# Attention steps of the second layer two slots earlier, and the join of near and far keys begun from the maxima

## The chip, the cores and the metric

The kernel is one program on one core of a Trainium2 chip. The metric is device time in microseconds (us) of one execution; the kernel before takes 2042.96 us, the median of three runs (2039.75 to 2043.41). A core has five engines with a queue each, working side by side and ordered by semaphores: TensorE (PE in the profile; its weight loads are PEld) for matrix products and transposes, VectorE (DVE), ScalarE (ACT), GpSimd (POOL) and SyncE (SP), which issues most DMA transfers. Matrix products end in PSUM, which the kernel uses as eight banks; the rest lies in SBUF.

## The reference, cut to what matters

A two-layer transformer over 512 tokens of width 1024 in float32. Each layer is attention and then a mixture of 32 experts, two per token. The change lies in the attention of the second layer: eight heads of width 64, each over three groups of keys with stride 1, 4 and 16, joined by the groups' log-sum-exp:

```python
def dilated_attention(h, w_q, q_gain, w_o, kv_blocks, rel_bias):
    q = rmsnorm((h @ w_q).reshape(b, s, B_NUM_GROUPS, N_HEADS, B_HEAD_DIM), q_gain[:, None, :])
    for g, (window, dil) in enumerate(B_GROUPS):
        kb, vb = kv_blocks[g]
        logits = jnp.einsum('bnqhd,bnkhd->bnhqk', qb, kb) * scale
        logits = jnp.where(mask[None, :, None], logits + bias[None, None], -jnp.inf)
        lse = jax.nn.logsumexp(logits, axis=-1)
        p = jnp.exp(logits - lse[..., None])
        o = jnp.einsum('bnhqk,bnkhd->bnqhd', p.astype(vb.dtype), vb)
        ...
    w = jax.nn.softmax(jnp.stack(lses, axis=2), axis=2)
    o = jnp.einsum('bsgh,bsghd->bshd', w.astype(outs[0].dtype), jnp.stack(outs, axis=2))
    return o.reshape(b, s, B_OUT_WIDTH) @ w_o

def hier_moe(h, w_group, b_group, w_expert, b_expert, w_gate, w_up, w_down):
    ...   # which experts a token goes to depends on h, so on the attention before it
```

## The kernel before

The second layer's attention has a loop of slots, n = 0, 1, 2, ..., written out by hand once for each of three engines (TensorE from L1775, ScalarE from L832, VectorE from L1175) with the same numbering; each engine's queue holds its part of slot n before its part of slot n + 1. What crosses engines is ordered by semaphores alone.

Slots 0 to 23 each project one tile (`tile`, L1720): a pair of heads (`hp`, four of them), a key group (three) and keys or queries. Behind it come the tile's square on ScalarE (L797), its mean by a product with a constant matrix (`tile_ms`, L1703, issued inside the next slot's tile), the reciprocal root as Ln and Exp (`tile_root`, L803 and L804) and on VectorE the product that leaves the normed tile (`tile_norm`, L1152, which signals `qk_t`).

Between the tiles run 16 steps, four per pair of heads. Steps 0 and 1 of a pair cover the near keys (group 0), steps 2 and 3 the far keys (groups 1 and 2, which share one softmax). Step x goes through
- `step_scores` (TensorE, L1742): query by key products into banks 3 and 4;
- `step_top` (VectorE, L1022): adds the bias, writes to `PB`, and leaves the row's extreme in `NM`, called the maxima here; signals `logits`;
- `step_exps` (ScalarE, L814): exponentials in place, with row sums into `SM`; signals `exps`;
- `step_turn` (TensorE, L1751): transposes the probabilities into banks 5 and 6;
- `step_probs`: copies bank 5 by ScalarE (L823) and bank 6 by VectorE (L1159);
- `step_values` (TensorE, L1771): products with the values into bank 7;
- `step_out` (ScalarE, L829), after every second step: copies bank 7.

The scores of step x wait for the maxima of step x - 1, since they use the same banks. In the kernel before, step x of pair hp has its scores in slot 6 hp + 6 + (x mod 4), its turn one slot later and its values two slots later. So the last pair's four steps stand in slots 24 to 29, after the last tile.

After the last step, the maxima `NM` and the sums `SM` are transposed (L1795, 16 transposes of 8 columns, into banks 0 to 3). VectorE takes from them the common extreme and two differences (L1194 to L1197), ScalarE their exponentials (L847), and VectorE the two weights per token and head (L1199 to L1204, with a reciprocal at L1202): the shares. TensorE spreads the shares over the channels (L1810), VectorE weighs the near and the far output with them (L1209 to L1211), and the output projection follows (L1822). Beside it the residual's gate is spread by two products with ones (L1801) and copied (L852).

Then come norm, routing and the experts. SyncE loads the weights of the experts in the order that routing has found (L426, behind a wait on the list of experts, L477, which VectorE writes at L1361), in a ring of six buffers of 2 MB.

Of the kernel before, what the change touches and what calls it, by code (L numbers as in the profile page):

```python
# [15 lines left out]
P = 128  # L16
# [5 lines left out]
H = 8  # L22
# [198 lines left out]
def program(nc, t, const, masks, buckets, out):  # L221
    with ExitStack() as ctx:
# [17 lines left out]
        C = sb("C", [P, C_END])  # L240
# [72 lines left out]
        N_TILES, N_STEPS = 24, 16  # L313
# [309 lines left out]
        def _(act):  # L623
# [30 lines left out]
            for l in range(LAYERS):  # L654
# [124 lines left out]
                else:  # L779
# [52 lines left out]
                    for n in range(N_TILES + 6):  # L832
                        if 1 <= n <= N_TILES:
                            tile_root(n - 1)
                        if n < N_TILES:
                            tile_square(n)
                        x = 4 * (n // 6 - 1)
                        if n >= 6:
                            at = n % 6
                            if at in (3, 5):  # L840
                                step_out(x + at - 2)
                            if 1 <= at <= 4:
                                step_probs(x + at - 1)
                            if at <= 3:
                                step_exps(x + at)
                    act.wait_ge(w_arg, 1)
                    act.activation(HT[0:H, 2048:3072], HT[0:H, 2048:3072], ACT.Exp).then_inc(w_exp, 1)  # L847

# [85 lines left out]
        def _(dve):  # L934
# [28 lines left out]
            for l in range(LAYERS):  # L963
# [159 lines left out]
                else:  # L1123
# [37 lines left out]
                    def step_top(x):  # L1161
                        hp, i = divmod(x, 4)
                        q = 4 * (i // 2) + 2 * (i % 2)
                        dve.wait_ge(*s["s_pe"](x + 1))
                        if x >= 2:
                            dve.wait_ge(*s["pt_pe"](x - 1))
                        for hd in range(2):
                            for cc in range(2):
                                lo = P if i == 0 and cc == 0 else 0
                                table = T3[:, 2 * hp + hd, (256 if i < 2 else 0) + lo:(512 if i < 2 else 256)]  # L1170
                                ins = top_of(PB[x % 2][:, hd, cc, lo:], bank[3 + hd][:, 256 * cc + lo:256 * (cc + 1)], table,
                                             NM[:, q + cc, 2 * hp + hd:2 * hp + hd + 1])
                        ins.then_inc(s["logits"].sem, 1)

                    for n in range(N_TILES + 6):  # L1175
                        if 1 <= n <= N_TILES:
                            tile_norm(n - 1)
                        x = 4 * (n // 6 - 1)
                        if n >= 6:
                            at = n % 6  # L1180
                            if 1 <= at <= 4:
                                step_probs(x + at - 1)
                            if at <= 3:
                                step_top(x + at)

# [11 lines left out]
                    dve.tensor_tensor(e1, za, nm1, ALU.subtract).then_inc(w_arg, 1)  # L1197
                    dve.wait_ge(w_exp, 1)
                    dve.tensor_tensor(za, e0, sm0, ALU.mult)  # L1199
                    step(dve.tensor_tensor(zb, e1, sm1, ALU.mult))  # L1200
                    step(dve.tensor_tensor(za, za, zb, ALU.add))
# [260 lines left out]
        def _(pe):  # L1462
# [39 lines left out]
            for l in range(LAYERS):  # L1502
# [152 lines left out]
                else:  # L1655
# [68 lines left out]
                    def step_scores(x):  # L1724
                        hp, i = divmod(x, 4)
                        pe.wait_ge(*s["qk_t"](6 * hp + (2 if i < 2 else 6)))
                        if x:
                            pe.wait_ge(*s["logits"](x))
                        else:
                            pe.wait_ge(*s["proj_free"](12))  # L1730
                        for cc in range(2):
# [6 lines left out]
                            for g, k0, w, to in parts:  # L1738
                                k, q = kq_tile(6 * hp + 2 * g), kq_tile(6 * hp + 2 * g + 1)
                                for hd in range(2):  # L1740
                                    r = slice(hd * DH, (hd + 1) * DH)
                                    ins = pe.matmul(bank[3 + hd][:, 256 * cc + to:256 * cc + to + w], q[r, c * P:(c + 1) * P],  # L1742
                                                    k[r, k0:k0 + w], start=True, stop=True)
# [31 lines left out]
                    for n in range(N_TILES + 6):  # L1775
                        if n < N_TILES:
                            tile(n)
                        elif n == N_TILES:
                            tile_ms(n - 1)
                        x = 4 * (n // 6 - 1)  # L1780
                        if n >= 6:
                            at = n % 6
# [6 lines left out]
                        if n == N_TILES + 4:  # L1789
                            pe.wait_ge(*s["qk_t"](N_TILES))  # L1790
                            pe.wait_ge(*s["logits"](N_STEPS))
                            for i, stat in enumerate((NM, SM)):
                                for q in range(8):
                                    b = bank[2 * i + q // 4]
                                    ins = pe.transpose(b[0:H, (q % 4) * P:(q % 4 + 1) * P], stat[:, q, :], ident)  # L1795
                            ins.then_inc(stat_pe, 1)
# [5 lines left out]
                    ins.then_inc(s["gate_pe"].sem, 1)  # L1802
                    pe.wait_ge(share, 1)
# [221 lines left out]
```

## Time and profile before

| | |
|---|---|
| median of three runs | 2042.96 us |
| time of the profiled execution | 2048.82 us |
| its span, first to last instruction | 2046.9 us |
| TensorE busy | 1748.3 us, 85% |
| VectorE busy | 541.4 us, 26% |
| ScalarE busy | 418.6 us, 20% |
| HBM traffic over the span | 276 GB/s |
| mean granted TensorE clock | 0.921 of full speed |

The profile is of one execution. Busy time is what an engine's instructions took, and a share of it is an average over stages that have different limits. The chain of waits follows the end of the program back to what released it; in it TensorE holds 66% of the span and DMA 24%. The granted clock has two levels in the rows, 1.00 (2.4 GHz) and 0.50 (1.2 GHz); values between are means over a stretch with both.

### The profile page before, as it was taken

The page shows a single profiled execution, that of the slowest core. Times are in us where ns is not written, and L with a number is a line of the kernel's source. Part 1 is how long each engine was busy: PE and PEld are TensorE (multiplying, and loading weights), DVE is VectorE, ACT ScalarE, POOL GpSimd, SP SyncE. Part 2 cuts the span into 40 slices and gives each one's busy share as a digit, 9 for nine tenths or more (in the row PEclk, how much of TensorE's full clock was granted, in tenths as well). Part 3 has the DMA queues.
Part 4 walks back from the last instruction along what each step waited for, and adds up shares of the span by engine and source line. Part 5 has one row for each costly group of instructions (what it writes and reads, how often), then busy time and mean ns, then how long its engine had stood idle before and what let it go on. Part 6 is the DMA issues. An engine that isn't in the chain of part 4 may idle for free.

```text
span 2046.9 us, 16908 instructions
## 1 busy us (share of the span) xinstructions
PE 1748.3 (85%) x6442; PEld 811.8 (40%) x6442; DVE 541.4 (26%) x1169; ACT 418.6 (20%) x1021; POOL 108.8 (5%) x110
## 2 busy tenths in 40 slices
PE   2999997869988898989498999978679988988894
PEld 0545554453333333333244454543533333333331
DVE  1575562340110111001466122224311101111112
ACT  2323353121111111111310234330211111111110
POOL 0000001010000010000000000010000000000000
PEclk9999997969999999989698999977679999999997
DMA  9872523029999999999666021120179999999995
GB/s 337 303 253 81 194 85 125 0 69 407 410 410 408 407 388 409 392 393 405 228 205 205 0 83 42 58 70 1 42 305 409 410 410 409 399 407 401 382 408 204
DMA packets 188981, 539.98 MB, mean 264 GB/s; under 512 B 15444, under 2 KB 52805, under 8 KB 188894
## 3 DMA queue, kind: packets, MB, share of 16 engines
q1 hardware_dynamic: 153536, 492.85, 62.1%
q0 software_dynamic: 14784, 28.38, 3.8%
q10 hardware_dynamic: 20574, 17.59, 2.8%
q8 instruction: 55, 0.90, 0.2%
q14 instruction: 32, 0.26, 0.0%
HBM read 536.64 MB, written 27.29 MB: 276 GB/s over the span
## 4 chain that ended last, share of the span: by engine, by line
PE 66%; DMA 24%; DVE 6%; ACT 2%; issue 1%; ACTq 1%; SPq 0%; POOLq 0%; DVEq 0%
PE psum L1903 22%; DMA ring<-in_moe_w_up_dram 20%; PE psum L1720 8%; PE psum L1537 8%; PE psum L1934 7%; PE psum L1592 3%; PE psum L1690 2%; PE psum L1822 1%; DVE W L998 1%; PE psum L1885 1%; DMA V<-expert_rows 1%; PE psum L1838 1%; PE psum L1566 1%; PE psum L1703 1%; PE psum L1483 1%
## 5 line engine op out<-in xcount | busy, mean ns | idle before, releaser
L1903 PE MATMUL psum<-ring,V 128*64 128x512 f32 (+1 forms) x2048 | 599.1, 629 | 89.8 <-DMA ring<-in_moe_w_up_dram 73.7
L1903 PEld LDWEIGHTS psum<-ring,V 128*64 128x64 f32 (+1 forms) x2048 | 224.1, 158 | 435.1 <-issue 435.1
L1934 PE MATMUL psum<-ring,V 128*64 128x512 f32 (+1 forms) x1024 | 290.0, 597 | 9.8 <-issue 7.3
L893 ACT ACTIVATE V<-psum,modall,scls 128x128 f32<-128x128 f32 x320 | 120.5, 456 | 495.0 <-PE psum L1885 495.0
L1934 PEld LDWEIGHTS psum<-ring,V 128*64 128x64 f32 (+1 forms) x1024 | 99.4, 150 | 147.8 <-issue 147.8
L998 DVE SCALAR_TENSOR_TENSOR W<-ring,cact,W 128x512 f32<-128x512 f32 (+1 forms) x224 | 138.5, 618 | 7.7
L1393 DVE SCALAR_TENSOR_TENSOR HT<-psum,slot_gate,XN 128x512 f32<-128x512 f32 x80 | 60.1, 751 | 270.0 <-PE psum L1934 270.0
L1377 DVE TENSOR_TENSOR V<-V,psum 128x512 f32<-128x512 f32 x40 | 27.5, 689 | 391.1 <-PE psum L1903 391.1
L1537 PE MATMUL psum<-HT,ring 128*128 128x512 f32 x256 | 115.7, 597 | 0.0
L902 ACT ACTIVATE V<-psum 128x512 f32<-128x512 f32 x40 | 23.9, 597 | 382.6 <-PE psum L1903 382.6
L1383 DVE COPY V<-psum 128x512 f32<-128x512 f32 x40 | 27.6, 691 | 277.3 <-PE psum L1914 277.3
L575 POOL DMA_INDIRECT expert_rows<-HT,dst x40 | 40.1, 1004 | 961.5 <-DVE HT L1393 961.5
L1720 PE MATMUL psum<-HT,ring 128*128 128x512 f32 x192 | 89.8, 612 | 0.0
L1720 PE MATMUL psum<-ring 128*128 128x512 f32 x192 | 86.9, 595 | 0.0
L1885 PE MATMUL psum<-C,V 128*128 128x128 f32 x320 | 54.5, 296 | 20.3 <-DMA V<-xn_scratch,tok 10.6
L1537 PEld LDWEIGHTS psum<-HT,ring 128*128 128x128 f32 x256 | 47.4, 190 | 54.8 <-issue 54.1
L1885 PEld LDWEIGHTS psum<-C,V 128*128 128x128 f32 x320 | 38.2, 148 | 73.3 <-issue 65.3
L1690 PE MATMUL psum<-ring 128*128 128x512 f32 x128 | 58.6, 612 | 0.0
L1537 PE MATMUL psum<-ring,HT 128*128 128x512 f32 x128 | 57.3, 597 | 0.0
L1152 DVE SCALAR_TENSOR_TENSOR ring<-psum,colV,W 128x512 f32<-128x512 f32 x24 | 23.8, 990 | 118.5 <-ACT W L804 118.5
L1720 PEld LDWEIGHTS psum<-HT,ring 128*128 128x128 f32 x192 | 36.8, 196 | 45.0 <-issue 44.6
L1720 PEld LDWEIGHTS psum<-ring 128*128 128x128 f32 x192 | 35.8, 190 | 43.0 <-issue 42.6
(258 smaller groups left out, 1460.4 us busy)
## 6 DMA issues: line engine op xcount, KB each, us to landing
ring<-in_moe_w_gate_dram SPq DMA_DIRECT2D x64, 2048.0 KB, 19.5
ring<-in_moe_w_up_dram SPq DMA_DIRECT2D x64, 2048.0 KB, 20.7
ring<-in_moe_w_down_dram SPq DMA_DIRECT2D x64, 2048.0 KB, 19.5
ring<-in_ada_w_dram SPq DMA_DIRECT2D x16, 2048.0 KB, 13.9
ring<-in_ada_w_dram ACTq DMA_DIRECT2D x16, 1024.0 KB, 5.4
ring<-in_a_w_qkv_dram SPq DMA_DIRECT2D x8, 1024.0 KB, 12.4
ring<-in_kv_ada_w_dram SPq DMA_DIRECT2D x4, 2048.0 KB, 15.3
V<-expert_rows SPq DMA_DIRECT2D x8, 1024.0 KB, 7.1
```

Of the source, the lines that this page charges most:

```text
L575: pool.indirect_dma_start(ys_d[l], bass.IndirectOffsetOnAxis(ap=rows, axis=0), HT[:, b * D:(b + 1) * D], None, bounds_check=last_row, oob_ ...
L893: ins = act.activation(V[:, 2 * D + b * D + k * P:2 * D + b * D + (k + 1) * P], bank[0][:, q * P:(q + 1) * P], ACT.Identity, bias=mod[:, 2 ...
L998: ins = dve.scalar_tensor_tensor(acc, w[:, k, :], cact[:, k:k + 1], acc, ALU.mult, ALU.add)
L1383: dve.tensor_copy(V[:, 5 * D + b * HALF:5 * D + (b + 1) * HALF], bank[1][:, :]).then_inc(s["hid_t"].sem, 1)
L1393: dve.scalar_tensor_tensor(HT[:, to], bank[6 + hf], slot_gate[:, COLS[p]:COLS[p] + 1], gf_row[:, hf * HALF:(hf + 1) * HALF], ALU.mult, ALU ...
L1537: ins = pe.matmul(bank[n % 2], rows, cols, start=(k == 0), stop=(k == KC - 1))
L1592: ins = pe.matmul(bank[WO_BANK[u]], OT0[k][:, c * P:(c + 1) * P], w3[:, k, :], start=(k == 0), stop=(k == KC - 1))
L1690: ins = pe.matmul(bank[u % 4], rows, slot3(n)[:, k, :], start=(k == 0), stop=(k == KC - 1))
L1720: ins = pe.matmul(bank[n % 2], w[:, k, (hp % 2) * P:(hp % 2 + 1) * P], (HTQ if kind else ht3)[:, k, :], start=(k == 0), stop=(k == KC - 1))
L1885: ins = pe.transpose(bank[0][:, q * P:(q + 1) * P], V[:, b * D + k * P:b * D + (k + 1) * P], ident)
L1903: ins = pe.matmul(bank[2 + 2 * i + b][half * w:(half + 1) * w, :], V[:, col:col + w], slot3(x)[:, k, :], start=(k == 0), stop=(k == KC - 1))
L1934: ins = pe.matmul(bank[6 + hf][half * w:(half + 1) * w, :], V[:, col:col + w], slot3(x, 4)[:, k, hf * HALF:(hf + 1) * HALF], start=(k == 0 ...
```

## The change

All steps move two slots forward: step x of pair hp has its scores in slot 6 hp + 4 + (x mod 4). The loops end at slot 24, and what is left of the last steps is written out behind them. The scores of step 15 no longer wait for the maxima of step 14: they go to banks 0 and 1 instead of 3 and 4 and stand right behind the scores of step 14. The transposes of the statistics are split: the maxima as soon as step 15's are known, the sums once its exponentials are done. VectorE's and ScalarE's part of the join moves between the copies of steps 14 and 15. Ahead of the wait for the shares, three products of ones with 512 columns of constants are added on TensorE, whose result nobody reads.

```diff
-                    for n in range(N_TILES + 6):
-                        if 1 <= n <= N_TILES:
+                    for n in range(N_TILES + 1):
+                        if n >= 1:
                             tile_root(n - 1)
...
-                        x = 4 * (n // 6 - 1)
-                        if n >= 6:
-                            at = n % 6
+                        x, at = 4 * ((n + 2) // 6 - 1), (n + 2) % 6
+                        if x >= 0:
...
+                    step_exps(15)
+                    step_out(13)
+                    step_probs(14)
                     act.wait_ge(w_arg, 1)
                     act.activation(HT[0:H, 2048:3072], HT[0:H, 2048:3072], ACT.Exp).then_inc(w_exp, 1)
+                    step_probs(15)
+                    step_out(15)
...
+                    step_top(15)
...
                     dve.tensor_tensor(e1, za, nm1, ALU.subtract).then_inc(w_arg, 1)
+                    step_probs(14)
+                    dve.wait_ge(stat_pe, 2)
                     dve.wait_ge(w_exp, 1)
                     dve.tensor_tensor(za, e0, sm0, ALU.mult)
                     step(dve.tensor_tensor(zb, e1, sm1, ALU.mult))
+                    step_probs(15)
...
-                        if x:
+                        if x == 0:
+                            pe.wait_ge(*s["proj_free"](12))
+                        elif x < 15:
                             pe.wait_ge(*s["logits"](x))
-                        else:
-                            pe.wait_ge(*s["proj_free"](12))
...
-                                    ins = pe.matmul(bank[3 + hd][:, 256 * cc + to:256 * cc + to + w], q[r, c * P:(c + 1) * P],
+                                    ins = pe.matmul(bank[(3, 4, 0, 1)[hd + 2 * (x == 15)]][:, 256 * cc + to:256 * cc + to + w], q[r, c * P:(c + 1) * P],
...
+                    def stats(i, stat):
+                        for q in range(8):
+                            ins = pe.transpose(bank[2 * i + q // 4][0:H, (q % 4) * P:(q % 4 + 1) * P], stat[:, q, :], ident)
+                        ins.then_inc(stat_pe, 1)
+
...
+                    step_scores(15)
+                    step_values(13)
+                    pe.wait_ge(*s["logits"](N_STEPS))
+                    stats(0, NM)
+                    step_turn(14)
+                    pe.wait_ge(*s["exps"](N_STEPS))
+                    stats(1, SM)
+                    step_values(14)
+                    step_turn(15)
+                    step_values(15)
...
+                    for _ in range(3):
+                        pe.matmul(bank[5], ones, C[:, 0:512], start=True, stop=True)
                     pe.wait_ge(share, 1)
```

TensorE's queue from the last tile on, before (L1720 and L1703 are a tile and its mean, L1742 scores, L1751 a turn, L1771 values):

```order
L1720 MATMUL psum<-ring 128x512 x6
L1771 MATMUL psum<-W,V 64x128 x8
L1703 MATMUL psum<-W,C 128x512
L1742 MATMUL psum<-ring 128x128 x2
L1742 MATMUL psum<-ring 128x256 x2
L1751 MATMUL psum<-C,ring 128x128 x6
L1742 MATMUL psum<-ring 128x256 x4
L1771 MATMUL psum<-W,V 64x128 x6
L1751 MATMUL psum<-C,ring 128x128 x8
L1742 MATMUL psum<-ring 128x128 x8
```

The same place in the changed kernel, from the end of tile 22 on (its lines: L1727 and L1710 tile and mean, L1749 scores, L1758 turn, L1778 values):

```order
L1727 MATMUL psum<-HT,ring 128x512 x6
L1749 MATMUL psum<-ring 128x128 x2
L1749 MATMUL psum<-ring 128x256 x2
L1727 MATMUL psum<-ring 128x512 x2
L1710 MATMUL psum<-W,C 128x512
L1727 MATMUL psum<-ring 128x512 x6
L1758 MATMUL psum<-C,ring 128x128 x6
L1749 MATMUL psum<-ring 128x256 x4
L1710 MATMUL psum<-W,C 128x512
L1778 MATMUL psum<-W,V 64x128 x6
L1758 MATMUL psum<-C,ring 128x128 x8
L1749 MATMUL psum<-ring 128x128 x16
```

The scores and the turn of step 12 and the scores of step 13 now stand ahead of the last mean, among tiles, and the scores of steps 14 and 15 are one run of sixteen.

TensorE's queue from there to the shares, before (L1795 statistics, L1801 gate, L1810 shares spread):

```order
L1771 MATMUL psum<-W,V 64x128 x8
L1751 MATMUL psum<-C,ring 128x128 x8
L1742 MATMUL psum<-ring 128x128 x8
L1771 MATMUL psum<-W,V 64x128 x8
L1751 MATMUL psum<-C,ring 128x128 x8
L1795 MATMUL psum<-C,W 8x128 x16
L1771 MATMUL psum<-W,V 64x128 x8
L1801 MATMUL psum<-T,C 128x512 x2
L1810 MATMUL psum<-HT,W 128x512 x8
```

And in the changed kernel (L1784 statistics, L1814 gate, L1817 the three added products, L1825 shares spread):

```order
L1778 MATMUL psum<-W,V 64x128 x8
L1784 MATMUL psum<-C,W 8x128 x8
L1758 MATMUL psum<-C,ring 128x128 x8
L1784 MATMUL psum<-C,W 8x128 x8
L1778 MATMUL psum<-W,V 64x128 x8
L1758 MATMUL psum<-C,ring 128x128 x8
L1778 MATMUL psum<-W,V 64x128 x8
L1814 MATMUL psum<-T,C 128x512 x2
L1817 MATMUL psum<-C 128x512 x3
L1825 MATMUL psum<-HT,W 128x512 x8
```

The first half of the statistics has moved ahead of the turns and values of the last two steps, and the added products stand between the gate and the shares.

VectorE's queue of the join in the changed kernel (L1163 is the copy of a step, L1198 to L1211 the join, as L1194 to L1204 before):

```order
L1198 COPY HT<-psum 8x512
L1199 TENSOR_TENSOR HT<-HT,psum 8x512
L1200 TENSOR_TENSOR HT<-HT,psum 8x512
L1201 TENSOR_TENSOR HT<-HT,psum 8x512
L1163 COPY W<-psum 128x512
L1205 TENSOR_TENSOR HT<-HT,psum 8x512
L1206 TENSOR_TENSOR HT<-HT,psum 8x512
L1163 COPY W<-psum 128x512
L1208 TENSOR_TENSOR HT<-HT 8x512
L1209 RECIPROCAL HT<-HT 8x512
```

Before, both copies stood ahead of the join's first operation; now they stand inside it.

## Rows read from the trace of the kernel before

**Rows 1.** Waits of SyncE's DMA queue: who, for whom, total us, times, longest.

```profile
SPq L477 <- DVE eid L1361: 146.8, 1, 146.8
```

**Rows 2.** Busy us of each engine per stretch, granted clock, DMA share, GB/s.

```profile
1123.00:1349.00 226.00, 226.00 (x847) 110.44 (x847) 47.70 (x133) 78.80 (x184) 0.00 (x0) 0.99 0.15 48
...
1354.00:1444.00 90.00, 66.80 (x231) 35.06 (x232) 39.78 (x79) 19.52 (x51) 6.07 (x7) 0.75 0.02 4
...
1500.00:2000.00 500.00, 449.49 (x1697) 180.30 (x1699) 53.26 (x74) 70.88 (x175) 35.99 (x36) 0.96 1.02 404
```

**Rows 3.** Chain that ended last, loop: start, us, what.

```profile
1297.35 0.86 PE psum L1742 x8
...
1306.12 0.66 PE psum L1751 x6
1306.78 1.06 PE psum L1742 x8
...
1332.52 5.15 PE psum L1720 x12
...
1348.47 1.07 PE psum L1703 x2
```

**Rows 4.** Timeline, end of loop to shares: start, us, engine, line, [idle before <-releaser].

```profile
1349.57 0.69 ACT L803 ACTIVATE W<-psum,C 128x512 f32<-128x512 f32 x1
...
1350.95 1.09 DVE L1152 SCALAR_TENSOR_TENSOR ring<-psum,colV,W 128x512 f32<-128x512 f32 x1 [6.11 <-ACT W L804]
...
1362.24 1.97 PE L1751 MATMUL psum<-C,ring 128*128 128x128 f32 x8 [2.20 <-ACT ring L814]
...
1364.14 2.08 PE L1742 MATMUL psum<-ring 64*128 64x128 f32 x16
...
1366.27 0.43 DVE L1022 CUSTOM_DVE_ANT_0 ring<-psum,T 128x256 f32<-128x256 f32 x1 [1.33 <-PE psum L1742]
...
1367.77 0.51 ACT L814 ACTIVATE ring<-ring,W 128x256 f32<-128x256 f32 x1 [2.92 <-DVE W L1022]
...
1369.90 1.09 PE L1751 MATMUL psum<-C,ring 128*128 128x128 f32 x8 [2.02 <-ACT ring L814]
...
1377.61 3.50 PE L1795 MATMUL psum<-C,W 128*8 128x128 f32 x16
...
1377.81 0.69 DVE L1159 COPY W<-psum 128x512 f32<-128x512 f32 x1 [3.29 <-PE psum L1751]
...
1381.21 0.68 DVE L1194 COPY HT<-psum 8x512 f32<-8x512 f32 x1 [2.13 <-PE psum L1795]
...
1382.21 1.07 ACT L829 ACTIVATE XN<-psum 128x512 f32<-128x512 f32 x1 [3.81 <-PE psum L1771]
...
1383.43 1.95 PE L1801 MATMUL psum<-T,C 128*128 128x512 f32 x4 [1.27 <-ACT XN L829]
...
1383.94 1.05 ACT L847 ACTIVATE HT<-HT 8x1024 f32<-8x1024 f32 x1 [0.66 <-DVE HT L1197]
...
1385.03 0.68 DVE L1199 TENSOR_TENSOR HT<-HT,psum 8x512 f32<-8x512 f32 x1 [1.12 <-ACT HT L847]
...
1391.75 2.92 PE L1810 MATMUL psum<-HT,W 8*128 8x512 f32 x3 [6.37 <-DVE HT L1204]
```

**Rows 5.** Timeline of the shares and the start of the output projection.

```profile
1395.56 0.69 DVE L1209 TENSOR_TENSOR HT<-XN,psum 128x512 f32<-128x512 f32 x1 [3.87 <-PE psum L1810]
...
1396.88 0.69 DVE L1211 TENSOR_TENSOR HT<-HT,XN 128x512 f32<-128x512 f32 x1
...
1407.87 29.70 PE L1822 MATMUL psum<-ring,HT 128*128 128x512 f32 x64 [2.10 <-DVE HT L1211]
```

**Rows 6.** Busy us per stretch, after the loop; the clock is the third number from the end.

```profile
1350.40:1355.00 4.60, 0.00 (x0) 0.00 (x0) 2.12 (x9) 2.38 (x9) 0.00 (x0) 0.87 0.88 363
1355.00:1367.50 12.50, 10.28 (x64) 8.18 (x66) 3.95 (x17) 3.16 (x10) 0.00 (x0) 0.50 0.00 0
...
1391.70:1405.80 14.10, 14.01 (x16) 5.14 (x16) 5.93 (x9) 0.00 (x0) 0.00 (x0) 0.50 0.00 0
```

More of the change, by code:

```diff
@@ L1170, in step_top @@
                                 table = T3[:, 2 * hp + hd, (256 if i < 2 else 0) + lo:(512 if i < 2 else 256)]
-                                ins = top_of(PB[x % 2][:, hd, cc, lo:], bank[3 + hd][:, 256 * cc + lo:256 * (cc + 1)], table,
+                                ins = top_of(PB[x % 2][:, hd, cc, lo:], bank[(3, 4, 0, 1)[hd + 2 * (x == 15)]][:, 256 * cc + lo:256 * (cc + 1)], table,
                                              NM[:, q + cc, 2 * hp + hd:2 * hp + hd + 1])
                         ins.then_inc(s["logits"].sem, 1)
-                    for n in range(N_TILES + 6):
-                        if 1 <= n <= N_TILES:
+                    for n in range(N_TILES + 1):
+                        if n >= 1:
                             tile_norm(n - 1)
-                        x = 4 * (n // 6 - 1)
-                        if n >= 6:
-                            at = n % 6
+                        x, at = 4 * ((n + 2) // 6 - 1), (n + 2) % 6
+                        if x >= 0:
                             if 1 <= at <= 4:
@@ L1773, in step_values @@
                         ins.then_inc(s["o_pe"].sem, 1)
-                    for n in range(N_TILES + 6):
+                    def stats(i, stat):
+                        for q in range(8):
+                            ins = pe.transpose(bank[2 * i + q // 4][0:H, (q % 4) * P:(q % 4 + 1) * P], stat[:, q, :], ident)
+                        ins.then_inc(stat_pe, 1)
+                    for n in range(N_TILES + 1):
                         if n < N_TILES:
                             tile(n)
-                        elif n == N_TILES:
+                        else:
                             tile_ms(n - 1)
-                        x = 4 * (n // 6 - 1)
-                        if n >= 6:
-                            at = n % 6
+                        x, at = 4 * ((n + 2) // 6 - 1), (n + 2) % 6
+                        if x >= 0:
                             if at >= 2:
@@ L1788, in _ @@
                                 step_scores(x + at)
[L1789 to L1796, printed above, removed]
+                    step_scores(15)
[8 more added lines that the diff above has]
+                    step_values(15)
                     pe.wait_ge(*s["diag"](1))
```

## The prediction

> **What bounds the kernel now.** I read the queue of the expert loads first, then busy time by stretch, then the chain that ended last, then the timeline of the stretch that the change touches. The first question is whether an earlier end of attention is worth anything at the end of the program. The queue that issues the expert weights waited 146.8 us for one instruction, the list of experts that routing writes [rows 1]; meanwhile the DMA engines did next to nothing (share 0.02 between 1354 and 1444 us), and from 1500 to 2000 us they were full (1.02, 404 GB/s) [rows 2]. So the last stage is a stream of fixed length that starts when routing is done, and routing follows attention with nothing else beneath it. A microsecond won before the output projection should be a microsecond at the end.
>
> Inside attention there are two regimes. From 1123 to 1349 us TensorE was busy 226.00 of 226.00 us, at granted clock 0.99 [rows 2]: projections of tiles, with steps sprinkled between. After that no projections are left, and the last four steps (12 to 15) run as a bare chain over three engines: a step's scores, its maxima on VectorE, its exponentials on ScalarE, its turn on TensorE, then the next step's scores. From the turn of step 13 at 1362.24 to that of step 14 at 1369.90 is 7.7 us [rows 4]. Then come the transposes of the statistics (L1795), ten VectorE operations with one Exp among them, and the stage of shares (L1810), which begins at 1391.75 and ends where the output projection begins, at 1407.87 [rows 4, 5]. I work out by how much that last instant moves.
>
> **What the loop takes over.** Moved two slots forward, the loop now also holds the scores of step 12, the turn of step 12 and the scores of step 13: 0.86 + 0.66 + 1.06 = 2.6 us by the same three pieces one pair of heads earlier [rows 3]. TensorE has no gap there, so this is paid in full: the square mean of tile 23, which began at 1348.4 [rows 3], begins at 1351.0. In return their maxima and exponentials lie beside projections.
>
> The other steps move with them, at no cost in the loop: the same instructions on an engine that is always busy. What could stall is a step's third scores, which now need the tile normalised in the same slot. ScalarE first has the exponentials of the scores that end as the slot begins, so with maxima (1.5), exponentials (2.1), root (1.4) and norm (1.1) [rows 4] the tile is ready 6.1 us into the slot. The scores stand behind a tile of 18 pieces of 0.43 (5.15 for 12 [rows 3]), a turn of 1.1 (1.09 at 1369.90 [rows 4]) and a values step, which I take alike: 9.9. The slack is 3.8 us, so I cost it at nothing.
>
> **The chain to the first statistics.** The last slot has no tile to cover it. Scores 13 end at 1351.0; maxima 1.5 (from 1366.27 to 1367.77 [rows 4]); exponentials 2.1 (1367.77 to 1369.90); behind them on ScalarE the root of tile 23, 1.4 (1349.57 to 1350.95), and its norm on VectorE, 1.1; then scores 14, which need that norm. They took 2.08 at half clock, and 1.06 in the loop [rows 4, 3]. Scores 15 go into two other banks at once and lie beside the maxima of step 14, so two sets of maxima follow each other, 3.0; then eight of sixteen statistics transposes, 1.75 of 3.50. At full clock: 1351.0 + 1.5 + 2.1 + 1.4 + 1.1 + 1.1 + 3.0 + 1.75 and small gaps = 1363.1. At half clock scores 14 take 1.0 more and scores 15 hold back the second maxima by 0.6: 1364.7. Before, all sixteen were done at 1381.1 [rows 4]. This part wins 16.4 to 18.
>
> **From there to the shares.** Before, 10.6 us passed from the statistics (1381.1) to L1810 (1391.75). Now the copies of steps 14 and 15 stand between the same VectorE operations, and a chain on TensorE runs beside them: values 14, turn 15, values 15, ScalarE's out copy, the gate's two matmuls (L1801), and three new matmuls of 512 columns which L1810 must wait for. With full clock, counted from the statistics: four VectorE operations 2.8 (1381.21 to 1383.94), copy 0.7, values 14 and turn 15 at 1.1 each: 5.75; copy 0.7: 6.5, and from there VectorE needs 5.4 more to the shares (6.7 from 1385.03 to 1391.75 less the two products of 1.3 that now fit before): 11.9, so 1375.0. TensorE meanwhile: values 15 1.1, out copy 1.1, L1801 2.0 [rows 4], and the three matmuls, six pieces of 0.43: it is free 13.4 after the statistics, at 1376.5. VectorE's new wait, for the second statistics, ends about 2.9 after the first, ahead of the Exp (3.9), and holds nothing behind it. GpSimd's gate diagonal and its small router loads hang on the last maxima and come earlier with them. So **the new matmuls are late next**, by 1.5 us; the shares are no longer the last to arrive. At half clock throughout (turn 1.97 [rows 4], a piece 14.01/16 = 0.88 [rows 6]): 3.5 + 2.0 + 2.0 + 0.7 + 2.0 + 1.1 + 3.5 + 5.3 = 20.2 after 1364.7, 1384.9. The trace has no row with these gaps. Of the two ends I take 1378.0, near the upper clock, since TensorE has no gap over 1.5 us in the new order from scores 14 on, while the clock fell in a gap of 4.6 us [rows 6]. Against 1391.75 that is 13.75 won, between 6.9 and 15.3.
>
> **The stage of shares.** Before it took 1391.75 to 1407.87, 16.1 us, with sixteen pieces of 0.88 at clock 0.50 and VectorE's three operations per pair (2.0, 1395.56 to 1397.57 [rows 5]) behind the last. If all ran at full clock, 1.75 us per pair, VectorE would set the pace: 1.75 + four times 2.1 = 10.1. The middle case is a clock that is full at the start, since ten pieces of 512 columns stand right ahead, and falls: two pairs at 1.75, two at 3.5: 3.9 + 3.5 + 3.5 + 2.1 = 13.0. I take this one, because TensorE was busy 14.01 of 14.10 us in these very matmuls and the clock stayed at 0.50, the lower level, 1.2 of 2.4 GHz [rows 6]: they do not hold it up. 3.1 won. The output projection I leave at its length; it had the lower clock in its first pieces and will again.
>
> The Trainium skill says in "TensorE: Matmul & The Clock Gate", section "What's actually happening", that the throttled clock is the default and that recent activity of the engine releases it. Taken at its word, an engine as busy as in L1810 should have been released; this trace disagrees (0.50 throughout), so I keep the row. By the rule the stage would be the 10.1 us case, and the result that of the first rival.
>
> **Sum.** 13.75 + 3.1 = 16.85, so 17 us. In the profiled execution's terms the span goes from 2046.9 to 2030, its time from 2048.8 to 2032. The median of the three runs, 2042.96, lies 5.9 below the profiled time, and the same 17 us give **2026**.
>
> **Rivals.**
> 1. The clock stays full from scores 14 through the shares and into the output projection. For it: the ten pieces ahead of L1810. Against it: the 0.50 in L1810. L1810 starts at 1376.5, takes 10.1, and the projection's first five pieces save 0.45 each: 1407.9 - 1386.6 + 2 = 23 won, 2020.
> 2. The clock falls in the gap before scores 14 and stays at half. For it: it stayed at 0.50 from 1355 to 1367.5 though TensorE was busy 10.28 of 12.5 us [rows 6]. Then L1810 starts at 1384.9, and with 16.1 for the stage 7 are won: 2036. If the clock comes back only at the new matmuls, the stage takes 13.0 and 10 are won: 2033, which I take for this rival.
> 3. The expert stream hides everything, as it would if its loads were already flowing: 2043. Against it the 146.8 us of waiting and the empty DMA engines [rows 1, 2].
> 4. Slower: the third scores in slots 6, 12 and 18 wait for the norm. Only lateness beyond the slack of 3.8 counts, and it decides when three stalls eat 17 us, that is when each norm is 9.5 us late. At 10.8 late: 3 x 7 = 21 lost against 17 won, 2047. Against it: ScalarE was busy 78.80 of 226 us in the loop [rows 2], so little can pile up.
> 5. The change does not move what it says. The order of instructions shows the steps two slots earlier, so this is no more than a part of rival 3.
>
> **How the numbers follow.** Forecast 0.55, rival 1 0.15, rival 2 0.22, rival 3 0.05, rival 4 0.03. A difference under 0.2%, 4.1 us, is about what a measurement of this kernel cannot tell from none; the three runs lie 3.7 apart. Rivals 1 and 2 and the forecast are all faster: 0.92. Same is rival 3: 0.05. Slower is rival 4: 0.03. The range takes in rival 1 with 2 us for the spread of runs, 2018, and rival 2 at its far end, 2036. Left out are rivals 3 and 4 and little more, 0.1 to 0.2 in all.
>
> **What would show it.** In the profile after: TensorE without a gap up to scores 13, ending near 1351; scores 14 and 15 together at about 1357; the first statistics done between 1363 and 1365; the first L1810 matmul behind the new matmuls, not behind VectorE, near 1378, and its pieces going from 0.43 to 0.88 within the stage; the projection at about 1391; the expert list 17 us earlier and the DMA stream as long as before. The forecast is wrong if the DMA stream does not start earlier by what attention won, if L1810 runs wholly at one clock, or if scores wait inside the loop.

## The result, and the profile after

The changed kernel takes 2025.22 us, the median of four runs (2024.93 to 2028.22); the kernel before, beside it, 2042.07 us. The ratio is 0.9922, 95% interval 0.9905 to 0.9939. In a later batch (five rounds) the changed kernel took 2029.45 against 2042.43, ratio 0.9939, 0.9918 to 0.9959. The forecast was 2026: 17 us won; measured are 16.9 and 13.0.

The profiled execution has a span of 2026.4 us, 20.5 less than before, but not all of that belongs to the change: the tile loop, ahead of which the two kernels are the same, began at 1120.7 instead of 1123.1. So I compare stretches that begin with the loop's first tile. All numbers are us, read from the timelines; "shares" is the first product that spreads them, "projection" the first product of the output projection, "list" VectorE's write of the list of experts:

| from the first tile to | before | after | after, second profile |
|---|---|---|---|
| last square mean | 225.3 | 228.4 | 228.6 |
| first shares product | 268.7 | 254.0 | 254.3 |
| projection | 284.8 | 267.3 | 267.5 |
| list | 371.4 | 354.1 | 354.3 |
| end of span | 923.8 | 905.7 | 908.2 |

Of the 17.5 us won at the projection, 17.3 are still there at the list and 18.1 (in the second profile 15.6) at the end. In the thirteen profiles of this document the list is written between 345.6 and 371.4 us after the first tile, and the end follows 550.8 to 554.3 us behind it, early list or late. So a microsecond at the list is one at the end, give or take 2 us.

Busy time per stretch in the profile after (columns as in [rows 2], the clock third from the end), and the queue of the expert loads, which answer to [rows 2] and [rows 1]:

```profile
1121.00:1349.00 228.00, 228.00 (x866) 111.56 (x865) 49.28 (x142) 81.64 (x193) 0.00 (x0) 0.99 0.14 47
```

```profile
SPq L477 <- DVE eid L1368: 127.2, 1, 127.2
```

TensorE still has no gap in the loop, so no scores waited there. The loads waited 127.2 us for the list instead of 146.8, 19.6 less: the stream starts earlier by the 17.3 us won up to the list, and by the 2.4 us that the loop began earlier.

The timeline after the loop, which answers to [rows 4, 5] (start, us, engine, line; L1710 square mean, L803 root, L1758 turn, L1156 norm, L1749 scores, L1026 maxima, L1784 statistics, L1163 copy of a step, L1198 to L1211 the join, L1814 gate, L1817 the added products, L1825 shares, L1216 to L1218 their use on VectorE, L1837 projection):

```profile
1349.04 1.12 PE L1710 MATMUL psum<-W,C 128*128 128x512 f32 x2
...
1352.64 0.67 ACT L803 ACTIVATE W<-psum,C 128x512 f32<-128x512 f32 x1
1352.79 1.09 PE L1758 MATMUL psum<-C,ring 128*128 128x128 f32 x8 [1.81 <-ACT ring L814]
...
1354.00 1.09 DVE L1156 SCALAR_TENSOR_TENSOR ring<-psum,colV,W 128x512 f32<-128x512 f32 x1 [3.38 <-ACT W L804]
...
1355.15 3.57 PE L1749 MATMUL psum<-ring 64*128 64x128 f32 x32 [1.27 <-DVE ring L1156]
...
1357.28 0.42 DVE L1026 CUSTOM_DVE_ANT_0 ring<-psum,T 128x256 f32<-128x256 f32 x1 [1.66 <-PE psum L1749]
...
1360.30 1.04 PE L1784 MATMUL psum<-C,W 128*8 128x128 f32 x8 [0.55 <-DVE W L1026]
...
1367.05 0.69 DVE L1163 COPY W<-psum 128x512 f32<-128x512 f32 x1 [0.44 <-DVE HT L1206]
...
1370.22 1.95 PE L1814 MATMUL psum<-T,C 128*128 128x512 f32 x4 [1.25 <-ACT XN L829]
...
1372.02 2.74 PE L1817 MATMUL psum<-C 128*128 128x512 f32 x6
...
1372.34 0.67 DVE L1211 TENSOR_TENSOR HT<-HT 8x512 f32<-8x512 f32 x1
1374.68 3.69 PE L1825 MATMUL psum<-HT,W 8*128 8x512 f32 x8
...
1378.77 7.14 PE L1825 MATMUL psum<-HT,W 8*128 8x512 f32 x8 [0.39 <-DVE HT L1218]
...
1382.54 0.69 DVE L1216 TENSOR_TENSOR HT<-XN,psum 128x512 f32<-128x512 f32 x1 [1.90 <-PE psum L1825]
...
1388.02 29.95 PE L1837 MATMUL psum<-ring,HT 128*128 128x512 f32 x64 [2.10 <-DVE HT L1218]
```

The order of the forecast is all there. Scores 14 wait for the norm of tile 23 and not for the maxima; scores 15 follow in one run with them (x32 pieces); the statistics are done at 1361.3. VectorE has the shares at 1373.0, but the first shares product starts at 1374.7, with no wait named: it stood behind the added products. Its stage is 13.3 us long instead of 16.1. Busy time around it shows the clock:

```profile
1355.00:1358.40 3.40, 3.25 (x30) 3.25 (x32) 1.74 (x9) 0.00 (x0) 0.00 (x0) 0.51 0.02 5
1358.40:1374.68 16.28, 11.96 (x96) 7.55 (x94) 12.53 (x23) 8.81 (x23) 6.16 (x7) 1.00 0.08 10
1374.68:1378.80 4.12, 3.73 (x10) 1.44 (x9) 2.06 (x4) 0.00 (x0) 0.00 (x0) 1.00 0.00 0
1378.80:1385.90 7.10, 7.10 (x8) 2.41 (x8) 3.78 (x6) 0.00 (x0) 0.00 (x0) 0.50 0.01 2
```

The clock was down for 3.4 us under the scores, came back, held at full through the join and the first half of the shares, and fell again in the middle of them, with TensorE busy 7.10 of 7.10 us.

### The profile page after: what moved, and what is told of

Its sections match the earlier page's. It is cut to its first block, busy times and chain, and to the rows that moved or that the text cites. A ratio compares the mean times of both kernels' runs of the same rounds, so it can differ in the third digit from the quotient of the medians.

```text
span 2026.4 us, 16919 instructions
## 1 busy us (share of the span) xinstructions
PE 1740.0 (86%) x6448; PEld 806.3 (40%) x6448; DVE 540.7 (27%) x1169; ACT 418.2 (21%) x1021; POOL 108.9 (5%) x110
## 4 chain that ended last, share of the span: by engine, by line
PE 66%; DMA 24%; DVE 5%; ACT 2%; issue 1%; ACTq 1%; POOLq 0%; SPq 0%; DVEq 0%
PE psum L1918 22%; DMA ring<-in_moe_w_up_dram 19%; PE psum L1727 8%; PE psum L1544 8%; PE psum L1949 7%; PE psum L1599 3%; PE psum L1697 2%; PE psum L1837 1%; PE psum L1900 1%; DVE W L1002 1%; PE psum L1853 1%; DMA ring<-in_moe_w_gate_dram 1%; PE psum L1573 1%; DMA V<-expert_rows 1%; PE psum L1591 1%
## 5 line engine op out<-in xcount | busy, mean ns | idle before, releaser
L1727 PE MATMUL psum<-HT,ring 128*128 128x512 f32 x192 | 89.9, 613 | 0.0
L1727 PE MATMUL psum<-ring 128*128 128x512 f32 x192 | 87.0, 596 | 0.0
L1727 PEld LDWEIGHTS psum<-HT,ring 128*128 128x128 f32 x192 | 36.8, 196 | 44.7 <-issue 44.3
L1156 DVE SCALAR_TENSOR_TENSOR ring<-psum,colV,W 128x512 f32<-128x512 f32 x24 | 23.7, 989 | 113.6 <-ACT W L804 113.6
L1727 PEld LDWEIGHTS psum<-ring 128*128 128x128 f32 x192 | 35.7, 190 | 42.8 <-issue 42.5
## 6 DMA issues: line engine op xcount, KB each, us to landing
ring<-in_kv_ada_w_dram SPq DMA_DIRECT2D x4, 2048.0 KB, 15.3
```

The lines of the kernel that those rows point to most:

```text
L1727: ins = pe.matmul(bank[n % 2], w[:, k, (hp % 2) * P:(hp % 2 + 1) * P], (HTQ if kind else ht3)[:, k, :], start=(k == 0), stop=(k == KC - 1))
```

## The experiments

Two questions were open: which part of the change earns what, and what decides the clock in the shares. Times are medians; ratios go against runs of the kernel before of the same batch, and need not equal the quotient of two medians. What a part is worth is read from the stretches of one profile per run.

**The changed kernel again.** 

> The changed kernel once more, beside the three variants of this batch. Theory A (the gain is what the last steps, the join and the shares won, 17 to 18 us): 16 to 18 us under the kernel before, about 2025. Theory B (part of the gain is drift of the stages ahead of attention, 2.4 us in the pair of profiles): a gain of 14 to 16.

2029.45 against 2042.43. The stretch to the projection repeats to 0.2 us (267.5), so attention's share was 17.5 and 17.3 in the two profiles; what varies lies outside it. The 13.0 is under both expected windows. Its profile was 1.4 us longer than before from the list to the end, and its loop began 5.4 earlier, without any change there. So the end shows the gain of the stretch plus or minus some us from elsewhere, as theory B supposed; the size of that is not explained.

**Without the added products.**

```diff
-                    for _ in range(3):
-                        pe.matmul(bank[5], ones, C[:, 0:512], start=True, stop=True)
```

> The three added products of 512 columns ahead of the shares are left out; all else is the changed kernel. Theory A (they are late by 1.7 us in the profile after, and the products of the shares cannot hold the clock whatever stands ahead of them): the shares start 1.7 us earlier, the clock falls earlier inside them; the stage from the first product of the shares to the output projection takes 13 to 15 us, and the total is within 2 us of the changed kernel, either way. Rival (the added products earn their keep by the clock): the clock is at its lower level for the whole stage, which then takes 16 us, and the total is 1 to 3 us slower than the changed kernel.

2026.68, ratio 0.9916 (0.9888 to 0.9944); 266.3 to the projection, 1.0 less than with them. TensorE's timeline (L1823 shares, L1835 projection) and the stretches around:

```profile
1369.38 1.96 PE L1814 MATMUL psum<-T,C 128*128 128x512 f32 x4 [1.25 <-ACT XN L829]
1372.23 11.67 PE L1823 MATMUL psum<-HT,W 8*128 8x512 f32 x16 [0.89 <-DVE HT L1211]
1386.00 4.64 PE L1835 MATMUL psum<-ring,HT 128*128 128x512 f32 x5 [2.10 <-DVE HT L1218]
```

```profile
1371.20:1374.80 3.60, 2.71 (x7) 1.22 (x7) 1.53 (x3) 1.08 (x2) 0.00 (x0) 0.98 0.00 0
1374.80:1384.00 9.20, 9.10 (x11) 2.94 (x9) 5.44 (x10) 0.00 (x0) 0.00 (x0) 0.50 0.00 0
```

The shares now wait for VectorE, the stage starts 1.6 us earlier (24.1 behind the last square mean, 25.6 with them), begins at full clock all the same, loses it earlier, and is 13.8 long instead of 13.3. Theory A holds for the stage; its total does not, being 2.8 under the 2029.45 of the changed kernel beside it, where at most 2 were expected. In the stretch, the added products cost 1 us where they stand.

**Added products in TensorE's gaps.** One ahead of the last values, one behind them, one behind the gate.

```diff
+                    def fill():
+                        pe.matmul(bank[4], ones, C[:, 0:512], start=True, stop=True)
+
+                    fill()
                     step_values(15)
+                    fill()
...
-                    for _ in range(3):
-                        pe.matmul(bank[5], ones, C[:, 0:512], start=True, stop=True)
+                    fill()
```

> The changed kernel with its three added products spread: one ahead of the last values, one behind them, one behind the gate. Theory A (they are late by 1.7 us where they stand): the first product of the shares starts with VectorE's last operation, 1.7 us earlier; the clock falls inside the stage as before, so the total is 1 to 2 us under the changed kernel. Rival (what counts is the clock at the start of the shares, and only products right ahead of them set it): no gain, or 1 to 2 us slower.

2024.25, ratio 0.9911 (0.9892 to 0.993). 24.1 from the last square mean to the shares, stage 13.7, 266.3 to the projection: 1.0 less than the changed kernel, near theory A, and the same as with none at all. They are free there, and buy nothing.

**Only the loop shift.** The change of the loops alone (`x, at = 4 * ((n + 2) // 6 - 1), (n + 2) % 6`, and loops that end at slot 27), with the old tail.

> The kernel before with its steps two slots earlier and nothing else: the scores of step 15 wait for the maxima of step 14, both statistics are transposed after the turn of step 15, the join follows the last copies, no added products. Theory A (parts add up): the first product of the shares starts 7 to 9 us after that of the changed kernel; 7 to 12 us faster than before, that is about half of the whole gain. Rival (the two steps in the loop are the whole change and the rest only polishes): 14 us or more faster than before.

2036.78, ratio 0.9969 (0.9955 to 0.9984). The shares start 34.4 behind the last square mean, 8.8 after the changed kernel's 25.6, as theory A said. But 278.4 to the projection is 6.4 won (5.3 between the medians), under its window of 7 to 12: the stage of shares was wholly at the lower clock, 16.1 us, as in the kernel before, so that only the earlier start counts. TensorE there (L1740 scores, L1749 turn, L1792 statistics, L1807 shares):

```profile
1354.68 2.08 PE L1740 MATMUL psum<-ring 64*128 64x128 f32 x16 [1.27 <-DVE ring L1151]
...
1362.34 2.05 PE L1740 MATMUL psum<-ring 64*128 64x128 f32 x16
...
1369.83 2.52 PE L1792 MATMUL psum<-C,W 128*8 128x128 f32 x16
...
1382.99 14.01 PE L1807 MATMUL psum<-HT,W 8*128 8x512 f32 x16 [6.41 <-DVE HT L1202]
```

Two steps fewer in the bare chain are a good third of the gain. The scores of steps 14 and 15 are still 7.7 us apart, and TensorE still idles 6.4 us ahead of the shares.

**Scores 15 behind the maxima of step 14.**

```diff
-                                ins = top_of(PB[x % 2][:, hd, cc, lo:], bank[(3, 4, 0, 1)[hd + 2 * (x == 15)]][:, 256 * cc + lo:256 * (cc + 1)], table,
+                                ins = top_of(PB[x % 2][:, hd, cc, lo:], bank[3 + hd][:, 256 * cc + lo:256 * (cc + 1)], table,
...
-                        elif x < 15:
+                        else:
                             pe.wait_ge(*s["logits"](x))
...
-                                    ins = pe.matmul(bank[(3, 4, 0, 1)[hd + 2 * (x == 15)]][:, 256 * cc + to:256 * cc + to + w], q[r, c * P:(c + 1) * P],
+                                    ins = pe.matmul(bank[3 + hd][:, 256 * cc + to:256 * cc + to + w], q[r, c * P:(c + 1) * P],
```

> The changed kernel with the scores of step 15 in banks 3 and 4 again, behind the maxima of step 14. Theory A (scores 15 lie beside the maxima of step 14): the first statistics are done 1.2 to 1.7 us later, counted from the last square mean of the loop, and all behind them as much later. Rival (VectorE is the bound there and scores 15 are hidden anyway): no shift, under 0.3 us.

2032.06, ratio 0.9948 (0.9931 to 0.9966). TensorE (L1749 scores, L1784 statistics, L1778 values, L1814 gate, L1825 shares):

```profile
1354.12 2.08 PE L1749 MATMUL psum<-ring 64*128 64x128 f32 x16 [1.27 <-DVE ring L1156]
1357.86 2.08 PE L1749 MATMUL psum<-ring 64*128 64x128 f32 x16 [1.66 <-DVE W L1026]
...
1361.50 1.04 PE L1784 MATMUL psum<-C,W 128*8 128x128 f32 x8
...
1366.05 1.09 PE L1778 MATMUL psum<-W,V 128*64 128x128 f32 x16 [1.39 <-issue]
...
1371.43 3.52 PE L1814 MATMUL psum<-T,C 128*128 128x512 f32 x4 [1.25 <-ACT XN L829]
...
1377.46 1.12 PE L1825 MATMUL psum<-HT,W 8*128 8x512 f32 x2
```

The first statistics are done 14.5 behind the last square mean instead of 12.3, so 2.2 later, above the window of theory A: both scores ran at the lower clock, 2.08 each. A second loss was not expected: the clock fell again at the start of the gate, which took 3.52 instead of 1.95, with the added products behind it:

```profile
1366.00:1371.20 5.20, 3.21 (x40) 2.62 (x40) 4.19 (x5) 2.00 (x3) 1.69 (x3) 1.00 0.19 29
1371.20:1374.80 3.60, 3.37 (x5) 1.52 (x6) 2.99 (x3) 0.09 (x1) 0.00 (x0) 0.53 0.00 0
```

To the projection 271.4, 4.0 more than the changed kernel: 2.2 from the scores and 1.6 from the gate's clock.

**The join where it was.** Both statistics behind the turn of step 15, both copies ahead of the join, the Exp behind the last out copy; the rest as changed.

> The changed kernel with the join where it was: both statistics after the turn of step 15, the copies of steps 14 and 15 ahead of the join, the Exp behind the last out copy. Theory A: VectorE has the shares about 4 us later, counted from the last square mean of the loop, and since the added products then no longer come last, the products of the shares start 2 us later; total 2 us slower than the changed kernel, a little more where the clock falls in the longer gap. Rival (the early join is hidden behind the last turns and values): the shares start within 0.5 us of the changed kernel.

2031.22, ratio 0.9946 (0.9933 to 0.9959). VectorE has the shares 28.6 behind the last square mean instead of 24.0, 4.6 later, near theory A's 4. The shares start 3.0 later, where 2 were expected, and their stage takes 15.3 since the clock fell within its first microsecond (L1816 added products, L1824 shares, L1836 projection; then the stretches):

```profile
1373.24 2.74 PE L1816 MATMUL psum<-C 128*128 128x512 f32 x6
1379.13 13.21 PE L1824 MATMUL psum<-HT,W 8*128 8x512 f32 x16 [3.15 <-DVE HT L1211]
1394.44 2.08 PE L1836 MATMUL psum<-ring,HT 128*128 128x512 f32 x2 [2.10 <-DVE HT L1218]
```

```profile
1379.13:1380.10 0.97, 0.97 (x2) 0.47 (x3) 0.00 (x0) 0.00 (x0) 0.00 (x0) 0.94 0.00 0
1380.10:1392.00 11.90, 11.90 (x15) 4.33 (x13) 5.93 (x9) 0.00 (x0) 0.00 (x0) 0.50 0.00 1
```

Here the added products end 3.15 us before the shares. To the projection 272.0, 4.6 more than the changed kernel, over twice the 2 of theory A; 2.0 of that lie in the stage, at the lower clock.

**Only the added products, in the kernel before.**

> The kernel before with only the three added products ahead of its wait for the shares. Theory A (they end 3.7 us before the shares there, and products of 8 rows do not hold the clock): the stage starts when it did, and takes 14 to 16.1 us; 0 to 2 us faster. Rival (they alone keep the stage at full clock): 13.3 us or less for the stage, 3 us or more faster.

2043.37, ratio 1.0004 (0.9991 to 1.0017), 284.75 to the projection against 284.80. The stage took 16.1. Nothing, as theory A said.

**The shares over 128 rows.** The last point is the clock in the shares. Their products read 8 rows of both operands, one per head. These runs read all 128, of which one operand's other 120 are zeroed; the sums are the same, and a piece is as long (eight take 3.69 us with 8 rows and 3.70 with 128, at full clock).

```diff
+                    pool.wait_ge(*s["qk_pe"](N_TILES))
+                    pool.memset(HT[:, 2048:3072], 0.0).then_inc(rows_zero, 1)
...
+                    dve.wait_ge(rows_zero, 1)
...
-                            ins = pe.matmul(bank[(4, 0)[hp % 2] + i], W[0:H, 2560 + hp * P:2560 + (hp + 1) * P],
-                                            HT[0:H, 2048 + S * i:2048 + S * (i + 1)], start=True, stop=True)
+                            ins = pe.matmul(bank[(4, 0)[hp % 2] + i], W[:, 2560 + hp * P:2560 + (hp + 1) * P],
+                                            HT[:, 2048 + S * i:2048 + S * (i + 1)], start=True, stop=True)
```

> The products of the shares use all 128 rows of both operands instead of 8: GpSimd zeroes the 120 further rows of the shares (one memset of 128 x 1024 after the last tile, one wait more on VectorE), the values are the same. Theory A (the clock fell in this stage because products of 8 rows do not hold it, however densely they follow each other): clock 1.00 through the stage, which takes 10.1 us instead of 13.3, and the first pieces of the output projection at full clock, 2 us more; 4 to 5 us faster than the changed kernel. Rival (the fall comes from the gaps between pairs, or from the time since the added products, not from the rows): the clock falls inside the stage as in the profile after, 13 us, total unchanged within 1 us.

2020.2, ratio 0.9903 (0.9878 to 0.9929): the stage took 10.0 us at clock 1.00 throughout (first line). To the projection 264.0, 3.3 less than the changed kernel, and 5.6 less to the list; the 9 us between the two medians of that batch are more than either can account for. The projection began at full clock, but 1.2 us into it lost it for 3.4 us (second line), so that part of theory A came only in part.

```profile
1368.37:1378.35 9.98, 7.50 (x17) 2.68 (x15) 7.72 (x12) 0.00 (x0) 0.00 (x0) 1.00 0.01 2
1379.50:1382.90 3.40, 3.40 (x5) 1.34 (x5) 0.00 (x0) 0.00 (x0) 0.00 (x0) 0.50 0.00 0
```

Next, 128 rows with the added products in the gaps.

> As the run with 128 rows, and of the three added products one stands in TensorE's gap ahead of the last values, one behind the last values and one, as before, behind the gate (they write another bank). Theory A: the shares start when VectorE has them, 1.7 us earlier, the clock is full throughout; 5 to 7 us faster than the changed kernel, about 2019. Rival (the added products must stand right ahead of the shares): the clock falls before the shares begin, and the gain over the changed kernel is under 3 us.

2021.29, ratio 0.9889 (0.9863 to 0.9915); 262.5 to the projection, stage 10.1, clock 1.00 into the projection. Its two parts add up to the 4.8 won against the changed kernel: the shares start 1.6 earlier and their stage is 3.2 shorter.

Then 128 rows and no added products at all.

> The changed kernel with the products of the shares over 128 rows and without the three added products. Theory A (it is the rows that hold the clock; the added products only cost time): from the start of the tile loop to the output projection 262.5 us, as the run with spread products and 128 rows had, 5 less than the changed kernel's 267.3; the stage of shares takes 10.1 to 11. Rival (both are needed: without added products the clock falls in the 1.2 us gap ahead of the shares): the stage takes 13 us or more, 265 us to the output projection.

2020.19, ratio 0.9894 (0.9876 to 0.9911); 262.1 to the projection, stage 10.1. The clock held without any added product (stage of shares, columns as above):

```profile
1369.37:1379.47 10.10, 7.61 (x17) 2.80 (x17) 7.72 (x12) 0.24 (x1) 0.00 (x0) 1.00 0.00 0
```

So the added products can go. Theory A holds. This version and the one ahead of it beat the kernel before by their ratios, which do not tell the two apart; to the projection this one, with less in it, is 5.2 us under the changed kernel. At the list it is 7.5 under it, since the projection now begins at full clock: its 64 pieces took 27.73 us instead of 29.95.

```profile
1379.47 27.73 PE L1839 MATMUL psum<-ring,HT 128*128 128x512 f32 x64 [2.10 <-DVE HT L1222]
```

Last, the 128 rows alone, in the kernel before.

> The kernel before with only the products of the shares over 128 rows instead of 8 (zeroed rows, the values are the same). There the stage began at the lower clock and stayed there, 16.1 us. Theory A (rows decide): the clock comes back inside the stage, which takes 12 to 14 us, and the output projection begins at full clock: 4 to 6 us faster than before. Rival (once down, the clock does not come back in a stage with waits between the pairs): the stage takes 16.1 us, no gain.

2035.07, ratio 0.9968 (0.9948 to 0.9987). In the kernel before the stage starts at the lower clock:

```profile
1388.70:1391.70 3.00, 2.98 (x4) 1.43 (x5) 0.00 (x0) 0.00 (x0) 0.00 (x0) 0.50 0.00 0
1391.70:1400.30 8.60, 6.12 (x13) 2.00 (x12) 7.73 (x12) 0.00 (x0) 0.00 (x0) 1.00 0.00 0
```

After 3 us of products with 128 rows the clock is back, where [rows 6] has it at 0.50 for 14.1 us with 8 rows. The stage takes 11.6, a little under theory A's 12 to 14, and 4.5 us are won at the projection. Against the kernel before, only the rows and the zeroing of them were changed, so the clock came back by them.

## Why the prediction was right

- **The bound.** That a microsecond at the projection is one at the list and at the end held: 17.5, 17.3, and 18.1 or 15.6. Rival 3 is out.
- **The loop.** Forecast 2.6 us later for the last square mean, measured 3.0 to 3.2, and 2.5 in the run with only the shift; no scores waited. Rival 4 is out. Where the further half microsecond comes from stays open.
- **The chain to the first statistics.** Forecast 12.1 behind that mean at full clock and 13.7 at half; measured 12.3. Two errors cancel in it. The scores ran at the lower clock, 3.57 for both, so that the first maxima began 8.2 behind the mean, 1.0 later than in the full-clock sum. And the eight transposes took 1.04, not 1.75: the 3.50 of [rows 4] that I halved for the full-clock sum had run at the lower clock, as this stretch of the kernel before shows (clock 0.52).

```profile
1377.61:1381.10 3.49, 3.49 (x20) 1.97 (x19) 1.28 (x2) 0.60 (x1) 3.06 (x5) 0.52 0.26 42
```

- **Rival 2.** The clock did fall ahead of scores 14, as rival 2 has it, but it was back by 1358.4, behind the scores, and not only at the added products.
- **From the statistics to the shares.** The forecast said that the added products would come last, by 1.5; it was 1.7 (1373.0 and 1374.7). Its full-clock sum, 13.4 us, is what was measured, 13.3. The step that was mis-sized is the choice between the ends: I took 1378.0, 27.0 behind the mean, where 25.5 (the upper clock) was right; measured 25.6. The lead of the shares' start came to 14.7, not 13.75. The half-clock sum adds up to 20.1 and not 20.2, which changes nothing. But the reason given for the upper clock, no gap over 1.5 us, does not carry it: with scores 15 behind the maxima of step 14, TensorE had no gap over 1.4 us from the statistics on, and the clock fell at the gate all the same. So the choice near the upper clock was right in part by luck.
- **The stage.** Forecast 13.0 with the clock full for two pairs and half for two; measured 13.3, with the fall 4.1 us into it. So 2.8 won, not 3.1. That products of 8 rows do not hold the clock was right, as the runs with 128 rows show. That it would fall behind just two pairs had no row behind it: it fell 2.6 us into the stage without the added products and within the first microsecond with the late join. So the close fit of the size is luck. Rival 1 would have had 10.1; that came only when the products had 128 rows. The Trainium skill ("TensorE: Matmul & The Clock Gate", section "What's actually happening") has the clock follow how busy the engine has been recently. Taken at its word, as the prediction does, this gives the 10.1 too; the stage with 8 rows, 13.3 us long, disagrees.
- **Sum.** 14.7 + 2.8 = 17.5 against the forecast's 16.85: two errors of opposite sign, each under a microsecond.

One reason in it did not hold. I let the stage start at full clock "since ten pieces of 512 columns stand right ahead". The six pieces of the added products are not needed for it: without them the clock was full at the start too, and the stage only 0.4 longer. The change got its gain despite them.

The parts, at the projection: the shift alone won 6.4; taking away the early scores costs 4.0 and taking away the early join 4.6, each with a loss of clock in it; the added products cost 1.0. These overlap, so they do not sum to 17.5. What moves the time of a whole execution by several us around the same attention (the tile loop began between 1114.3 and 1123.1 in these profiles) stays open.

## What to carry to other kernels

When a pipelined loop runs out of the work that covers its steps, start its steps earlier so that fewer are left bare, and look for a wait on a buffer (here two banks) that strings the last ones together. A product that is issued only to keep an engine busy is worth trying in an existing gap first, and worth leaving out once: here the wait that it replaced was the cheaper one. Cost a stage at both clock levels, say which one its own products hold, and look up at which level a row ran before taking its time as a price. Where products of few rows lose the clock, try them with the other rows zeroed: here that won more than the added products could.

## What the runs showed of the hardware

In these runs, products that use 8 of the 128 rows did not hold TensorE's upper clock, though they followed each other without a gap: 0.50 for 14.1 us with TensorE busy 14.01 [rows 6], and a fall from 1.00 to 0.50 inside the stage after, with TensorE busy 7.10 of 7.10 us behind it. The same products over 128 rows, with zeros, ran at 1.00 for 10.1 us, though TensorE was busy only 7.61 of them, and where the clock was down it was back after 3.0 us. The Trainium skill ("TensorE: Matmul & The Clock Gate", section "What's actually happening") ties the clock to how busy the engine has been recently. The stages with 128 rows agree with that; those with 8 do not, if busy means that products follow each other.

Not shown is what happens between 8 and 128 rows, and whether the number of rows counts or what stands in them. Nor are 8 rows the only way to lose the clock: it also fell for 3.4 us in the output projection behind one of the stages with 128 rows, with TensorE busy 3.40 of 3.40 us, and at the start of the gate with scores 15 behind the maxima of step 14. The cause of these two falls stays open.
